# A decoder trunk's mixture of experts: 32 experts in 26 passes, with weights laid out and loaded in 8 KB pieces

## What is computed

```python
pg = softmax(ht @ rg_w + rg_b); g_val, g_idx = top_k(pg, 1)         # 1 of 4 groups
le = logits of the 8 experts of that group
pe = softmax(le); e_val, e_idx = top_k(pe, 2); e_val /= sum(e_val)   # 2 of 8 experts
for each group o:
    hid = silu(ht @ w_gate[o, e]) * (ht @ w_up[o, e])                # 1024 -> 256
    out += (hid * coef) @ w_down[o, e]                               # 256 -> 1024
```

## Time and profile before

| | |
|---|---|
| median of three runs | 1217.24 us |
| the profiled execution | 1217.08 us, span of its instructions 1215.1 us |
| TensorE busy in it | 1078.8 us (89%) |
| VectorE, ScalarE, GpSimd busy | 491.6, 283.1, 190.1 us |
| moved by DMA | 163.03 MB in 112695 packets |
| of these under 2 KB | 94135 packets |

### The profile page before, as it was taken

One profiled execution on the slowest core, in us unless ns is written; L12 is line 12 of the kernel. 1 busy time (PEld: TensorE's weight loads), 2 busy tenths in 40 slices (PEclk: granted clock), 3 DMA queues, 4 the chain that ended last, 5 costly groups with the idle time before them and its releaser, 6 DMA issues. The chain is left out here.

```text
span 1215.1 us, 13911 instructions
## 1 busy us (share of the span) xinstructions
PE 1078.8 (89%) x5135; PEld 636.1 (52%) x5135; DVE 491.6 (40%) x1149; ACT 283.1 (23%) x645; POOL 190.1 (16%) x226
## 2 busy tenths in 40 slices
PE   6999999756987699999999999279999999999970
PEld 4434787655436466676664555145455455454430
DVE  3568340386026576666642222722122122122114
ACT  3200111301013676666541000100110110110113
POOL 3000000151011321101110000112322322222210
PEclk9999999977998999999999999669999999999995
DMA  9110100043000550000003243527999999899937
GB/s 250 70 38 3 70 1 0 14 95 70 0 10 10 115 169 2 2 2 1 2 2 114 112 168 126 190 77 256 328 309 309 303 304 313 277 298 299 304 79 276
DMA packets 112695, 163.03 MB, mean 134 GB/s; under 512 B 26487, under 2 KB 94135, under 8 KB 108471
## 3 DMA queue, kind: packets, MB, share of 16 engines
q1 hardware_dynamic: 102528, 144.36, 36.9%
q0 software_dynamic: 10112, 17.92, 6.1%
HBM read 148.40 MB, written 29.44 MB: 146 GB/s over the span
## 5 line engine op out<-in xcount | busy, mean ns | idle before, releaser
L1753 PE MATMUL banks<-shared,xt 128*128 128x512 f32 x512 | 226.8, 596 | 2.6 <-DVE xt L1792 1.7
L1753 PEld LDWEIGHTS banks<-shared,xt 128*128 128x128 f32 x512 | 95.6, 192 | 111.4 <-issue 110.1
L1771 PE MATMUL banks<-shared,hidt 128*128 128x512 f32 x256 | 115.2, 593 | 0.8 <-ACT hidt L1781 0.8
L1428 PE MATMUL banks<-wout,shared 128*128 128x512 f32 x256 | 112.7, 594 | 0.5 <-PEq L1161 0.5
L356 PE MATMUL banks<-x,wring 128*128 128x512 f32 x256 | 112.0, 594 | 0.9 <-DVE x L397 0.9
L1797 DVE SCALAR_TENSOR_TENSOR hid_e<-act_g,slot_coef,banks 128x256 f32<-128x256 f32 x32 | 15.4, 481 | 222.9 <-ACT act_g L1777 222.9
L1209 ACT ACTIVATE shared<-shared,low 128x640 f32<-128x640 f32 (+7 forms) x128 | 92.8, 729 | 2.6 <-DVE low L1296 2.1
L1259 PE MATMUL banks<-consts,shared 128*128 128x128 f32 x528 | 77.8, 282 | 4.4 <-ACT shared L1209 3.6
L356 PEld LDWEIGHTS banks<-x,wring 128*128 128x128 f32 x256 | 47.9, 190 | 60.0 <-issue 58.0
L1259 PEld LDWEIGHTS banks<-consts,shared 128*128 128x128 f32 x528 | 56.0, 141 | 43.8 <-issue 38.2
L1428 PEld LDWEIGHTS banks<-wout,shared 128*128 128x128 f32 x256 | 47.6, 190 | 55.2 <-issue 55.2
(11 more groups left out here) (315 smaller groups left out, 1266.1 us busy)
## 6 DMA issues: line engine op xcount, KB each, us to landing
shared<-in_exp_w_down SPq DMA_DIRECT2D x32, 1024.0 KB, 14.4
shared<-in_exp_w_gate SPq DMA_DIRECT2D x32, 1024.0 KB, 11.7
shared<-in_exp_w_up SPq DMA_DIRECT2D x32, 1024.0 KB, 17.6
shared<-in_x SPq DMA_DIRECT2D x8, 512.0 KB, 7.5
wring<-in_w_in SPq DMA_DIRECT2D x2, 2048.0 KB, 8.6
x<-in_x SPq DMA_DIRECT2D x1, 4096.0 KB, 31.7
x_rows<-x SPq DMA_DIRECT2D x8, 512.0 KB, 2.6
xn_rows<-xn SPq DMA_DIRECT2D x8, 512.0 KB, 2.9
```

What stands on the lines that cost most here:

```text
L1428: ins = nc.tensor.matmul(psum[n % 4], src[:, i * P:i * P + P], m["wout"][:, k, half * 512:half * 512 + 512], start=k == 0, stop=k == KD - 1)
L1753: ins = nc.tensor.matmul(psum[2 + p], xt[:, p, k], wgu[:, b, k], start=k == 0, stop=k == KD - 1)
L1771: ins = nc.tensor.matmul(psum[6 + half], hidt[:, p, k], wd[:, b, k, half * 512:half * 512 + 512], start=k == 0, stop=k == 1)
```

## The change

The diff replaces `stage_route` and `stage_experts` by one block, `stage_moe`.

- The order of work is a fixed list made at build time (`plan`). Four fixed experts (0, 16, 1, 17) come first, one pass each. The other 14 experts of each half of the 32 are ranked at run time by their number of tokens. The eight with most tokens of each half have a pass each; the six with least tokens of one half are paired with those of the other half by rank, two experts in one pass, each with 64 of the 128 rows. That makes 4 + 16 + 6 = 26 passes. An expert with more tokens than its rows gets extra columns as before (up to 21).
- In a paired pass `pe_gu` and `pe_down` issue each matmul twice, once for each expert: 64 stationary columns, output in the lower or upper 64 partitions, 512 moving columns.
- There are five weight buffers, the fifth in `x1` (whose rows have been stored by then). Gate and up are two contiguous halves of their buffer (8 KB each a partition).
- The lists of the four fixed experts are made first (`first_hot`); the ranking and the other lists are made by VectorE in portions between the operations of passes 0 to 2 (`rest`), and TensorE makes the second product behind pass 2's transposes. Expert numbers of the ranked ones are read by SP from memory (`ids`) and each load takes its address from a register.
- GpSimd uses columns of `tok` directly, with no copy ahead of a gather or a scatter. A scatter waits for the one before it when the two passes share a half.
- The 32 passes of before were partly a loop on the engines; the 26 are written out.
- The constants grow by 312 columns. A few semaphores are shared, and one small tile has moved.

```diff
-UN = NG
-SLOT_TILES_EXTRA = 15
+UN, WBUFS = 4, 5
+FIXED = (0, 1, 16, 17)
+RANKED, FULL = E // 2 - 2, 8
+COLS = 4 + 2 * FULL + RANKED - FULL
+SLOT_TILES_EXTRA = 21
+OVER_IDS = 24
+LISTS_AT = 2
...
-        "before": (q[:, None] < q[None, :]) * 1.0,
+        "after": (q[:, None] < q[None, :]) - 1.0,
-        "place": np.broadcast_to(UN * (np.arange(E) % EPG) + np.arange(E) // EPG, (P, E)),
+        "tie": np.broadcast_to(E - 1.0 - np.arange(E), (P, E)),
+        "first": np.broadcast_to(np.repeat([4, 5], RANKED), (P, 2 * RANKED)),
+        "back": np.broadcast_to(np.repeat([8, 7], RANKED), (P, 2 * RANKED)),
+        "carry": np.broadcast_to((np.arange(E * NT) % NT > 0) * 1.0, (P, E * NT)),
...
-                if i < UN:
-                    load_down(nc, d, m, sp, EPG * i, i)
-                elif i < UN + 2:
-                    load_gate_up(nc, d, m, sp, EPG * (i - 2), i - 2)
+                if i < 4:
+                    load_down(nc, d, m, sp, loads[i][0][1], buffer_of(i))
+                elif i < 6:
+                    load_gate_up(nc, d, m, sp, loads[i - 4][0][1], buffer_of(i - 4))
...
+def plan():
+    half = E // 2
+    statics = [(c, [("fixed", e)], {e // half}) for c, e in enumerate(FIXED)]
+    statics = [statics[k] for k in (0, 2, 1, 3)]
+    singles = [(4 + 2 * r + h, [("ranked", h, r)], {h}) for r in range(FULL) for h in range(2)]
+    pairs = [(12 + r, [("ranked", h, r) for h in range(2)], {0, 1}) for r in range(FULL, RANKED)]
+    order = statics + [(singles if kind == "S" else pairs).pop(0) for kind in "SSSPSSPSSSPSSPSSPSSPSS"]
+    assert not singles and not pairs and len(order) == COLS
+    passes, loads = [], []
+    for col, experts, halves in order:
+        passes.append((col, list(range(len(loads), len(loads) + len(experts))), halves))
+        loads += [(what, len(passes) - 1) for what in experts]
+    return passes, loads
+def buffer_of(j):
+    return (2, 3, 0, 1, 4)[j % WBUFS]
+def load_gate_up(nc, d, m, eng, e, b):
+    for k, name in enumerate(("exp_w_gate", "exp_w_up")):
+        src = d[name][0].rearrange("g e (p k) f -> (g e) p k f", k=KD)[bass.ds(e, 1)]
+        eng.dma_start(m["wgu"][b][:, k], src.rearrange("a p k f -> p (a k f)")).then_inc(m["w_in"][b], 16)
+def load_down(nc, d, m, eng, e, b):
+    src = d["exp_w_down"][0].rearrange("g e (p k) n -> (g e) p k n", k=2)[bass.ds(e, 1)]
+    eng.dma_start(m["wd"][b], src.rearrange("a p k f -> p (a k) f")).then_inc(m["wd_in"][b], 16)
...
+    def gather(n):
+        nc.gpsimd.indirect_dma_start(xg[:, n % UN], None, m["xn_rows"],
+                                     bass.IndirectOffsetOnAxis(m["tok"][:, passes[n][0]:passes[n][0] + 1], 0),
+                                     bounds_check=limits[0], oob_is_err=False).then_inc(x_in[n % UN], 16)
+    def scatter(gp, n):
+        at, _, halves = passes[n]
+        gp.wait_ge(s["y_act"], n + 1)
+        gp.wait_ge(s["y_dve"], n + 1)
+        if n and halves & passes[n - 1][2]:
+            gp.wait_ge(stored[(n - 1) % 2], 16 * ((n - 1) // 2 + 1))
+        nc.gpsimd.indirect_dma_start(m["x_rows"], bass.IndirectOffsetOnAxis(m["tok"][:, at:at + 1], 0), y[:, n % 2], None,
+                                     bounds_check=limits[0], oob_is_err=False, compute_op=ALU.add).then_inc(stored[n % 2], 16)
...
+    def pe_gu(pe, n, bufs, p):
+        pe.wait_ge(s["x_out"], 2 * n + 2)
+        w = P // len(bufs)
+        for k in range(KD):
+            for v, b in enumerate(bufs):
+                rows = slice(v * w, v * w + w)
+                ins = nc.tensor.matmul(psum[2 + p][rows].rearrange("p (a f) -> p a f", a=2), xt[:, p, k, rows], wgu[b][:, :, k],
+                                       start=k == 0, stop=k == KD - 1)
+        ins.then_inc(s["gu"], 1)
...
+                for v, b in enumerate(bufs):
+                    rows = slice(v * w, v * w + w)
+                    ins = nc.tensor.matmul(psum[6 + part][rows], hidt[:, p, k, rows], wd[b][:, k, part * 512:part * 512 + 512],
+                                           start=k == 0, stop=k == 1)
...
+            for j in (2, 3):
+                load_gate_up(nc, d, m, sp, loads[j][0][1], buffer_of(j))
+            sp.wait_ge(ids_ready, 1)
+            sp.wait_ge(m["x_stored"], 16 * NT)
+            for j in range(len(FIXED), len(loads)):
+                (_, h, r), n = loads[j]
+                e = sp.value_load(m["ids"][0:1, h * RANKED + r:h * RANKED + r + 1], min_val=0, max_val=E - 1)
+                if j >= WBUFS:
+                    sp.wait_ge(s["gu"], loads[j - WBUFS][1] + 1)
+                load_gate_up(nc, d, m, sp, e, buffer_of(j))
+                if j >= WBUFS:
+                    sp.wait_ge(s["y_done"], loads[j - WBUFS][1] + 1)
+                load_down(nc, d, m, sp, e, buffer_of(j))
+                if j == 2 * WBUFS:
+                    sp.dma_start(m["fg"][:], bc(d["final_g"], P, 0)).then_inc(fg_in, 16)
+            sp.wait_ge(fg_in, 16)
...
+            gp.wait_ge(first_ready, 1)
+            for n in range(len(FIXED)):
+                gather(n)
+            for n in range(NP):
+                if n + 2 < NP and n + 2 >= len(FIXED):
+                    if n + 2 == len(FIXED):
+                        gp.wait_ge(lists_ready, 1)
+                    gp.wait_ge(s["x_t"], 2 * (n + 2 - UN) + 2)
+                    gather(n + 2)
+                if n:
+                    scatter(gp, n - 1)
+            scatter(gp, NP - 1)
...
+            slots(first_hot, len(FIXED))
+            pe.wait_ge(x_in[0], 16)
+            pe.wait_ge(first_ready, 1)
+            pe_x(pe, 0, 0, False)
+            for n in range(NP):
+                bufs = [buffer_of(j) for j in passes[n][1]]
+                for j in passes[n][1]:
+                    pe.wait_ge(w_in[buffer_of(j)], 32 * nth[j])
+                pe_gu(pe, n, bufs, n % 2)
+                if n + 1 < NP:
+                    pe.wait_ge(x_in[(n + 1) % UN], 16 * gathered[n + 1])
+                    pe_x(pe, n + 1, (n + 1) % UN, True)
+                if n:
+                    for j in passes[n - 1][1]:
+                        pe.wait_ge(wd_in[buffer_of(j)], 16 * nth[j])
+                    pe_down(pe, n - 1, [buffer_of(j) for j in passes[n - 1][1]], (n - 1) % 2, n > 1)
+                pe_hid(pe, n, n % 2)
+                if n == LISTS_AT:
+                    pe.wait_ge(s["h_out"], n + 1)
+                    slots(tile_hot, COLS_ALL - len(FIXED))
...
+            row_hots("pos")
             chain(V.tensor_copy(pos[:].rearrange("p i e -> p (i e)"), psum[0][:, 0:NT * E]))
             chain(V.tensor_copy(cnt[:], psum[1][:, 0:E]))
-
-            tt(over[:], bc(cnt[:], 7, 2), bc(m["over"][:, 0:7], E, 1), ALU.is_gt)
-            reduce(nov[:], over[:], ALU.add)
-            chain(V.tensor_tensor_scan(ovend[:], m["ones"][:, 0:E], nov[:], 0.0, ALU.mult, ALU.add))
-            tt(ovbase[:], ovend[:], nov[:], ALU.subtract)
-            ts(ovbase[:], ovbase[:], float(E - 1), ALU.add)
-
-            for name, src in (("pos", None), ("eid", m["place"]), ("base", ovbase[:])):
-                tt(prod[:], pick[:], bc(pos[:], 2, 1) if src is None else bc(bc(src, NT, 1), 2, 1), ALU.mult)
-                reduce(ch[name][:], prod[:], ALU.add)
-            flat = "p k i -> p (k i)"
-            c = {n: t[:].rearrange(flat) for n, t in ch.items()}
-            tt(cm[:], bc(c["pos"], 7, 2), bc(m["over"][:, 0:7], 2 * NT, 1), ALU.is_ge)
-            reduce(c["m"], cm[:], ALU.add)
-            ts(c["t"], c["m"], float(-P), ALU.mult)
-            tt(c["pos"], c["pos"], c["t"], ALU.add)
-            tt(c["base"], c["base"], c["m"], ALU.add)
-            tt(c["base"], c["base"], c["eid"], ALU.subtract)
-            ts(c["t"], c["m"], 0.5, ALU.is_gt)
-            tt(c["base"], c["base"], c["t"], ALU.mult)
-            tt(c["eid"], c["eid"], c["base"], ALU.add)
-            ts(ch["val"][:], bc(m["token"], 2, 1), -float(DUMMY), ALU.add)
-            for k in range(2):
-                dve.wait_ge(m["xn_stored"][k], 16 * NT // 2)
-            hot = tile_hot[:, :, 1]
-            tt(hot, bc(c["eid"], tiles, 2), bc(m["row"][:, 0:tiles], 2 * NT, 1), ALU.is_equal)
-            tt(tile_hot[:, :, 0], hot, bc(c["val"], tiles, 2), ALU.mult)
-            for k in range(2):
-                tt(hot[:, k * NT:k * NT + NT], hot[:, k * NT:k * NT + NT], bc(m["coef"][:, :, k], tiles, 2), ALU.mult)
-            for n in range(0, 2 * NT, 4):
-                V.tensor_tensor(row_hot[:, n:n + 4], bc(c["pos"][:, n:n + 4], P, 2), bc(m["row"], 4, 1), ALU.is_equal
-                                ).then_inc(hot_ready, 1)
-
-            tt(ovt[:], bc(ovend[:], 16, 1), bc(m["row"][:, 0:16], E, 2), ALU.is_le)
-            reduce(ovid[:], ovt[:], ALU.add)
-            ts(ovid[:], ovid[:], float(E - 1), ALU.min)
-            chain(V.tensor_copy(ovid[:, 15:16], ovend[:, E - 1:E]))
-            chain(V.tensor_copy(m["ovid"], ovid[:]))
             dve.wait_ge(list_done, 1)
-            ts(list_f[:], psum[2][:, 0:tiles], float(DUMMY), ALU.add)
```

(126 more changed lines are left out.)

492 lines of the change are left out of this document (228 added, 264 removed).

## The result

Before 1217.3 us (four runs, 1214.9 to 1217.7), after 1172.95 us (1170.5 to 1175.8): ratio 0.964, 95% interval 0.961 to 0.967. Forecast 1161 us, range 1140 to 1195. The profiled execution after took 1170.98 us, with a span of 1169.2, so 45.9 us of span went (1215.1 - 1169.2).

The account below looks back on a forecast made before the run. Passes were taken as bound by TensorE, DMA about a tenth behind, then by DMA narrowly. -68.8 - 14.5 + 11.7 + 15 + 0.5 + 0.5 = -55.6 us from 1217.1 gave 1161 us, range 1140 to 1195.

Parts of the forecast that it names:

- the constants: Head of SP's load queue: 156 KB more constants to load, +0.5 us.
- A pair costs a single pass: Expert passes: two half tiles cost one whole, a paired pass takes 11.47 us, so six passes fewer give -68.8 us.
- Rival (c): Paired passes: half tiles don't run side by side at 512 columns, +62 us, DMA -15, 1208 us; chance 10%.
- No time for the change of form: Paired passes: switching between full and half tiles shows no time; 0.5 us booked for all six pairs.
- Start: Before the passes: lists of the first experts made first, first transposes at 789.6 instead of 804.2, -14.5 us.
- Lists: Behind pass 2: remaining list chain delays pass 3's gate and up, with slow clock and late gather, +11.7 us.
- Weights: Passes from 9 on: 20 loads at 7.8 us plus gathers and scatters take 198 us against 183.5, +15 us.
- a load follows a use: SP's weight loads: each waits in order for the buffer of five loads ago, so it cannot run ahead.
- Clock: TensorE: +1 us for a slow restart behind the lists; its fall at weight waits only in rival (d).
- rival (d): Passes behind pairs: starved TensorE falls to half clock again and again, slower than before, 1238 us; chance 4%.
- Rival (a): Expert passes: the DMA ring keeps up and TensorE still bounds, DMA term 0, 1146 us; chance 20%.
- Rival (b): Weight loads: larger pieces bring nothing beside gathers and scatters, 336 GB/s stays, +31 us, 1192 us; chance 18%.

Follow-up runs that it names:

- layout_only: The kernel before, with only gate and up laid out in contiguous 8 KB halves and loaded in 8 KB pieces, still 32 passes and four buffers: 1215.5 us, ratio 0.998.
- halves_apart: The changed kernel, with a pair's gate and up issued all for one expert, then all for the other, instead of in turn: 1183.0 us, ratio 0.971.
- sp_order: The changed kernel, with SP issuing loads by the time a buffer comes free, gate and up apart from down: 1167.9 us, ratio 0.960.
- small_downs: The changed kernel, with seven eighths of each ranked expert's down load left out, so results use what the buffers held: 1148.7 us, ratio 0.943.
- pieces_1k: The changed kernel, with gate and up interleaved in the buffer again and loaded in 1 KB pieces, still 26 passes: 1186.7 us, ratio 0.974.
- order_portions: The changed kernel with the edits of sp_order and portions together, pass order unchanged: 1158.5 us, ratio 0.952.
- all_three: The changed kernel with the edits of sp_order and portions, and a ranked-pass order that puts pairs earlier: 1153.4 us, ratio 0.947.
- lists_first: The changed kernel, with the ranking and all lists made as one chain ahead of the first pass: 1182.7 us, ratio 0.972.
- portions: The changed kernel, with more of VectorE's list chain in passes 0 and 1, and pass 2's row one-hots ahead of its result copy: 1163.9 us, ratio 0.957.

## Why the prediction was right

The bound was right: TensorE alone before (layout_only), TensorE and DMA after. The measured time is 12 us above the forecast: 7.1 us more of waits and clock, 3.9 more for the form of the pairs, 1.0 for the lists, 0.9 at the start and 0.1 for the constants, less 2.1 behind the last pass and the 1.2 in the mean, make 9.7 in the profiled execution, which is 2 us below the median. Point by point:

- *A pair costs a single pass.* Half tiles side by side held at 512 columns: 32 instructions in 7.0 us. Rival (c) is out, and halves_apart shows that it is the alternation that does it.
- *No time for the change of form.* Mis-sized: 0.73 us a pair. It shows between the groups, some 0.1 us at each change, for in the same timeline gate and up of a pair start 7.01 us ahead of the transposes, not 6.87, and these 1.00 ahead of down, not 0.88. The Trainium skill ("TensorEngine Tiling (Array Packing)", Key Properties), that a change of mode drains TensorE, fits with that; the price is small. No run takes drain apart from other costs of the half tiles.
- *Start.* Within 1 us. The chain could be placed from the old rows because its operations kept their durations.
- *Lists.* 12.7 for 11.7: idle 4.8 and the product at half clock throughout, 7.0 us, where I had it bound by VectorE's last one-hot. The gather I booked 2 us for did not wait.
- *Weights.* Mis-sized: 22.1 us with the clock for 15. The price of an expert was right: 33.47 MB in 0.772 of 106 us is 409 GB/s for a full share, 7.7 us an expert (I took 7.8). The step that failed is how I used "a load follows a use": I let SP issue each load at its release, and so the engines be full from pass 9 on. In fact a gate-and-up load whose buffer was free stood behind a down load that waited, 5.7 us ahead of pass 17 and again ahead of pass 20 and of pass 23 (released at 1020.4 and 1058.5, issued at 1026.10 and 1064.23), and sp_order gets 5 us back. That is less than the 7.1 us by which the term is off; no run takes apart which part of the rest is rate and which the order of the passes. I also had the waits behind pairs; they stand ahead of them, where two experts are wanted at once.
- *Clock.* Behind waits for weights I had put its fall only into rival (d), with small gaps. Two of the four waits, 7.6 and 5.8 us, brought it down for some microseconds; those of 1.1 and 3.1 did not. (d) itself, at 1238, is far off.
- Rival (a), no DMA term, is what small_downs shows: 1148.7 for 1146; the changed kernel isn't there. Rival (b) is out: its rate is that of pieces_1k (61.88 MB in 0.830 of 219 us, 340 GB/s for a full share), which is at 1187 instead of 1192, and the changed kernel's is 409. The 358 GB/s that the Trainium skill ("HBM Reference", Specifications) names as a core's share was passed: 375 GB/s over the 106 us from 905 to 1011, loads and gathers together, with one core running, which the page says can be.

Two things no run tells: what the fifth weight buffer is worth, since all kernels with 26 passes have it, and the time with other inputs, where an expert in a pair may have more than 64 tokens. Left over: the 2.1 us behind the last pass, of which 1.2 lie between the last scatter's issue and the first load of the last stage (10.7 us, before 11.8). No run tells the cause of those.

## What to carry to other kernels

Where TensorE is the bound and DMA a tenth behind, halving a pass's matmuls moves the bound at once; work out the bytes per pass for the densest stretch of the new order, not for the mean, and then look at the order in which one queue waits for two kinds of release. Half tiles of 64 columns can share the array at full speed if the two halves' instructions take turns. A chain of small vector operations costs nothing where it fits between an engine's own operations, and all its length where the tensor engine needs the last of it, so cut it by the idle time of each pass, not in equal portions.

## What I had not expected of the hardware

A DMA share of 1.00 doesn't fix the rate. From 855 to 895, order_portions and all_three both stand at 1.00 with the same 2.23 MB of gathers and scatters, but the loads, in pieces of the same size, run at 11.75 MB in 0.779 of 40 us in the one and 12.72 MB in 0.786 in the other, 377 and 405 GB/s for a full share. No run tells why.

How long TensorE waits doesn't by itself tell whether its clock falls. In the changed kernel the granted clock stayed at 2.4 GHz through the wait of 3.1 us at 1048 (1.00 from 1051.4 to 1055); in lists_first it was at 1.2 GHz behind a wait of only 2.2 us (0.50 from 1063.7 to 1067). And it was at 1.2 GHz (0.50, from 832.8 to 839.6) for the whole list product behind 4.8 us of idling, although TensorE was busy all that time. In portions, where it idled 0.7 us, the same product took 3.8 instead of 7.1 us.
